# Gated networks of a two-block transformer: activation halves side by side in one 512-column product, summed on VectorE

## The reference

```
ff1, ff2:    (silu(h @ w_gate) * (h @ w_up)) @ w_down                      # 1024 -> 2816 -> 1024
glu1, glu2:  gu = u @ w_up                                                 # 1024 -> 2 x 3072
             gate = causal_dwconv(gu[..., :3072], conv_w) + conv_b         # 3 taps over the positions
             (silu(gate) * gu[..., 3072:]) @ w_down
```

## Time and profile before

| | us |
|---|---|
| median of 3 runs | 1452.08 |
| lowest, highest | 1450.59, 1460.54 |
| profiled execution | 1451.2 |
| its span | 1448.4 |
| TensorE busy in the span | 1343.1 |
| VectorE busy | 917.4 |
| ScalarE busy | 669.9 |

### The profile page before, as it was taken

The page is one execution under the profiler, slowest core; times in us unless marked ns, Lnnn a source line. Parts: engine busy times, 40 slices in busy tenths (PEclk is TensorE's granted clock), DMA queues, the critical chain, the costliest instruction groups (busy, mean ns, idle before and its releaser), DMA issues.

```text
span 1448.4 us, 24980 instructions
## 1 busy us (share of the span) xinstructions
PE 1343.1 (93%) x10130; PEld 1264.0 (87%) x10130; DVE 917.4 (63%) x1373; ACT 669.9 (46%) x983; POOL 110.8 (8%) x98
## 2 busy tenths in 40 slices
PE   5999979988799999779999999899998879899998
PEld 5999979987799999768899999799997769899997
DVE  5655556666555555666666666689895654666665
ACT  5443444555443434545445444467532333544443
POOL 1000010000100000340000000014001620000000
PEclk9999999999999999989999999999998989999999
DMA  6655543630255555330455455344340004355551
GB/s 258 220 186 176 196 161 120 233 117 1 102 175 177 195 179 184 125 128 4 143 198 180 174 180 197 117 146 155 138 145 31 30 30 175 137 183 176 195 195 71
DMA packets 30313, 214.85 MB, mean 148 GB/s; under 512 B 3488, under 2 KB 3616, under 8 KB 4768
## 3 DMA queue, kind: packets, MB, share of 16 engines
q1 hardware_dynamic: 29808, 212.23, 41.9%
q0 software_dynamic: 432, 1.57, 0.3%
HBM read 212.74 MB, written 1.05 MB: 148 GB/s over the span
## 4 chain that ended last, share of the span: by engine, by line
PE 80%; DVE 11%; ACT 3%; POOL 3%; issue 2%; DMA 1%; SPq 0%; DVEq 0%; POOLq 0%; ACTq 0%
PE bank L445 71%; DVE w_lo L1599 2%; PE bank L607 1%; POOL stat L1486 1%; PE bank L461 1%; PE bank L651 1%; ACT w_hi L1053 1%; POOL stat L1457 1%; PE bank L620 1%; DVE arena L1991 1%; ACT aT_hi L1071 1%; DVE par L1989 1%; DVE aT_lo L1620 1%; ACT arena L1241 1%; DMA pos_i<-positions 1%
## 5 line engine op out<-in xcount | busy, mean ns | idle before, releaser
L1599 DVE TENSOR_TENSOR w_lo<-raw,w_hi 128x2048 fp32r<-128x2048 f32 x199 | 458.2, 2303 | 229.5 <-ACT w_hi L1053 229.3
L445 PE MATMUL bank<-aT_hi,w_hi 128*128 128x256 f32 x1728 | 492.5, 285 | 4.5 <-DVE aT_lo L1620 3.9
L445 PE MATMUL bank<-aT_hi,w_lo 128*128 128x256 f32 x1728 | 490.3, 284 | 0.0
L445 PE MATMUL bank<-aT_lo,w_hi 128*128 128x256 f32 x1728 | 490.2, 284 | 0.0
L1053 ACT ACTIVATE w_hi<-raw 128x2048 fp32r<-128x2048 f32 x199 | 380.2, 1911 | 133.1 <-PE bank L445 131.2
L445 PEld LDWEIGHTS bank<-aT_hi,w_hi 128*128 128x128 f32 x1728 | 332.9, 193 | 8.0 <-issue 4.1
L445 PEld LDWEIGHTS bank<-aT_lo,w_hi 128*128 128x128 f32 x1728 | 333.0, 193 | 1.5
L445 PEld LDWEIGHTS bank<-aT_hi,w_lo 128*128 128x128 f32 x1728 | 332.8, 193 | 0.0
L445 PE MATMUL bank<-w_hi,aT_hi 128*128 128x256 f32 x592 | 172.2, 291 | 4.4 <-DVE aT_lo L1620 1.8
L445 PE MATMUL bank<-w_hi,hT_hi 128*128 128x512 f32 (+2 forms) x464 | 171.7, 370 | 1.9 <-DVE hT_lo L1714 1.9
L445 PE MATMUL bank<-w_hi,hT_lo 128*128 128x512 f32 (+2 forms) x464 | 171.4, 369 | 0.0
(11 more groups left out here) (309 smaller groups left out, 1331.1 us busy)
## 6 DMA issues: line engine op xcount, KB each, us to landing
raw<-weights SPq DMA_DIRECT2D x199, 1024.0 KB, 4.9
post_gain<-post_gains POOLq DMA_DIRECT2D x3, 512.0 KB, 4.2
residual<-x SPq DMA_DIRECT2D x2, 512.0 KB, 4.1
out<-residual SPq DMA_DIRECT2D x2, 512.0 KB, 2.6
par<-params SPq DMA_DIRECT2D x1, 837.0 KB, 7.5
con<-consts SPq DMA_DIRECT2D x1, 520.0 KB, 10.6
con<-consts SPq DMA_DIRECT2D x1, 64.0 KB, 6.2
pos_i<-positions SPq DMA_DIRECT2D x1, 1.0 KB, 7.3
```

The costliest lines, as they stand in the source:

```text
L445: last = nc.tensor.matmul(to, lhsT, rhs, start=start and n == 0, stop=stop and n == 2)
L1599: nc.vector.tensor_tensor(w_lo[:, i % 3, :], raw[:, i % 3, :], w_hi[:, i % 3, :].bitcast(f32), ALU.subtract).then_inc(w_lo_done, 1)
```

## The change

`aT_hi` and `aT_lo` become the two halves of one buffer. For each part and k, the rounded weight `w_hi` is multiplied by both at once, a moving operand of 2 x 256 columns, so that one half of a bank holds the sum over k of `w_hi` with `aT_hi` and the other that with `aT_lo`; then `w_lo` with `aT_hi` is added into the first half. A tile is now 16 products of 512 columns and 16 of 256. Gate and up have a bank each, `bank[4 + 2 * (f % 2) + part]`, so two tiles instead of four hold banks in turn. VectorE adds the two halves of each bank with a reduction over two elements, to `f_sum` (gate) and `f_up` in SBUF; ScalarE's and VectorE's later steps read these in place of the bank. ScalarE waits for the gate's sum (`gate_summed`) instead of the tile's products, and TensorE, before it writes a bank again, for the sum of the tile two before it. Down products, splits, the order of the items and everything outside the four networks stay.

```diff
--- before.py
+++ after.py
@@ -77,8 +77,8 @@
         w_lo = sb("w_lo", [128, 3, ITEM], f32r)
 
 
-        aT_hi = sb("aT_hi", [128, 8, SEQ], f32r)
-        aT_lo = sb("aT_lo", [128, 8, SEQ], f32r)
+        aT = sb("aT", [128, 2, 8, SEQ], f32r)
+        aT_hi, aT_lo = aT[:, 0], aT[:, 1]
 
         with nc.sbuf_tensor("z_silu", [128, 8, 512], f32) as z_silu:
             pass
@@ -142,6 +142,8 @@
         f_gate = room(2, SEQ)
         f_tanh = room(2, SEQ)
         f_hid = room(2, SEQ)
+        f_sum = room(2, SEQ)
+        f_up = room(2, SEQ)
 
         used[0] = 0
         proj = room(2, 2816)
@@ -252,6 +254,7 @@
 
         rows_ready, turned, turned_hi, turned_lo = sem("rows_ready"), sem("turned"), sem("turned_hi"), sem("turned_lo")
 
+        gate_summed, up_summed = sem("gate_summed"), sem("up_summed")
         gate_scaled, gate_conv, gate_tanh = sem("gate_scaled"), sem("gate_conv"), sem("gate_tanh")
         hid_ready, hid_hi, hid_lo = sem("hid_ready"), sem("hid_hi"), sem("hid_lo")
         y_done = sem("y_done")
@@ -487,17 +490,19 @@
                 def tile(f, i, q):
 
                     pe.wait_ge(w_lo_done, i + 1 + 6 * q)
-                    if f0 + f >= 4:
-                        pe.wait_ge(hid_ready, f0 + f - 3 + 4 * q)
-                    to = bank[4 + f % 4]
                     for part in range(2):
+                        to = bank[4 + 2 * (f % 2) + part]
+                        if f0 + f >= 2:
+                            pe.wait_ge(up_summed if part else gate_summed, f0 + f - 1 + 4 * q)
                         for k in range(8):
                             at = 1024 * part + 128 * k
                             if f == 0 and part == 0 and k % 2 == 0:
 
                                 pe.wait_ge(turned_lo, turn(name) + k // 2 + 1)
-                            last = exact(to[:, 256 * part:256 * part + 256], weights(i, at, at + 128), left(k),
-                                         k == 0, k == 7)
+                            hi, lo = weights(i, at, at + 128)
+                            nc.tensor.matmul(to[:, :].rearrange("p (a c) -> p a c", a=2), hi, aT[:, :, k, :],
+                                             start=k == 0, stop=False)
+                            last = nc.tensor.matmul(to[:, 0:256], lo, aT_hi[:, k, :], start=False, stop=k == 7)
                     last.then_inc(item_done, 1)
 
                 def down(m, i, q):
@@ -1102,9 +1107,8 @@
                 pre_norm(name)
 
                 def tile(f, i, q):
-                    gate = bank[4 + f % 4][:, 0:256]
-                    act.wait_ge(item_done, i + 1 + 6 * q)
-                    tanh_of = gate
+                    tanh_of = gate = f_sum[:, f % 2, :]
+                    act.wait_ge(gate_summed, f0 + f + 1 + 4 * q)
                     if conv:
                         tap = P("ffn_conv")[:, 72 * (name == "glu2"):72 * (name == "glu2") + 72]
                         bias = P("ffn_bias")[:, 24 * (name == "glu2"):24 * (name == "glu2") + 24]
@@ -1691,8 +1695,12 @@
                 tap = tap.rearrange("p (f t) -> p f t", t=3)
 
                 def tile(f, i, q):
-                    gate, up = bank[4 + f % 4][:, 0:256], bank[4 + f % 4][:, 256:512]
+                    gate, up = f_sum[:, f % 2, :], f_up[:, f % 2, :]
                     g = f_gate[:, f % 2, :]
+                    dve.wait_ge(item_done, i + 1 + 6 * q)
+                    for part, to, done in ((0, gate, gate_summed), (1, up, up_summed)):
+                        halves = bank[4 + 2 * (f % 2) + part][:, :].rearrange("p (a c) -> p c a", a=2)
+                        nc.vector.tensor_reduce(to, halves, AX.X, ALU.add).then_inc(done, 1)
                     if conv:
 
                         dve.wait_ge(gate_scaled, f0 - 44 + f + 1 + 4 * q)
```

## The result

The changed kernel takes 1472.29 us, the median of four runs (1471.05 to 1474.22), against 1453.03 for the kernel before beside it: the ratio is 1.0128, with a 95% interval of 1.0102 to 1.0155. It is slower by 1.3%. The forecast was 1466 with a range of 1450 to 1484, and gave slower by over 1% a chance of 0.46 and no change that a measurement tells 0.47; its own sum, 13.9 us, is just under 1%. The profiled execution took 1474.22 us, span 1472.3, which is 23.9 more than the span of the kernel before.

What follows compares the result with a forecast made beforehand. The prediction took TensorE as today's bound, with VectorE becoming the bound of glu1 and glu2. Terms +9.1 + 1.0 + 6.65 + 1.7 - 4.0 - 0.6 = +13.9 us on the 1452.1 median gave 1466, range 1450 to 1484.

Steps and rivals of the forecast that it cites:

- VectorE becomes the bound of the convolved networks: In glu1 and glu2, sums lengthen VectorE's tile from 5.95 to 7.64 us, its pair to 17.49, over TensorE's 16.58.
- TensorE's wait: In glu1 and glu2, TensorE waits for w_lo some 0.9 us a pair.
- Rival 1: Convolved networks: sums hidden, looped tile 7.0 us, TensorE stays the bound; -8 us in all, 1444; chance 0.08.
- rival 2: Convolved networks: sums dearer, 1.04 us each, pair 18.2 us; total 1488; chance 0.11.
- rival 4: Convolved networks: index work overlaps the first sum, no clock terms; tiles 7.4, pairs 17.0 us; total 1453; chance 0.15.
- the pitches of rows 2: TensorE's gate and up products: 227.5 and 120.0 ns by width, saving 12.5 ns per k, 0.20 us a tile.
- Rival 3: TensorE's alternating stream has no gain, plain networks save nothing: 1474 us, or 1472 by the skill's rule; chance 0.10.
- ff2: forecast -4.0: Network ff2: TensorE stays the bound, 22 tiles save 0.20 us each, -4.4; later last hT_lo costs +0.4.
- ff1: forecast -0.6: Network ff1: bank wait +1.1, clock +1.7, 19 tiles saving 3.8, end +0.4; together -0.6 us.
- The wait of tile 2 for its bank: In ff1, tile 2 waits for tile 0's gate sum, starting at 32.05: +1.1 us, plus +1.7 for the clock.
- glu1: forecast +10.1: Network glu1: VectorE's longer tiles delay the last down product by 9.1 us; slow-clock products there add +1.0.
- glu2: forecast +8.35: Network glu2: VectorE's longer tiles delay the last down product by 6.65 us; the clock after TensorE's idle adds +1.7.

Runs made afterwards that it cites:

- experiment 4: Changed kernel with its sums, banks and waits kept, but three products of 256 columns per k again instead of one of 512 and one of 256: 1479.57 us, ratio 1.0177.
- experiment 5: Changed kernel plus a third VectorE reduction of 512 constant values per tile, after hT_lo, with nothing waiting for it: 1498.75 us, ratio 1.0321.
- experiment 11: The change in the even tile of each pair only; the odd tile keeps three 256-column products and no sum: 1449.39 us, ratio 0.9987.
- experiment 9: Changed kernel with each weight transfer after the first three cut to its first 16 columns: 1470.87 us, one run.
- experiment 7: Changed kernel with the two halves of aT side by side for every k, so the 512-column operand is one piece: 1474.57 us, ratio 1.0135.
- experiment 12: Changed kernel with each bank's eight 512-column products first, then its eight of 256, so widths don't alternate: 1470.99 us, ratio 1.0126.
- experiment 1: The change in ff1 and ff2 only, glu1 and glu2 as in the kernel before: 1452.69 us, ratio 1.0002.
- experiment 3: Changed kernel's products and two banks without the VectorE sums, later steps reading each bank's first half: 1449.35 us, ratio 0.9978.
- experiment 6: Changed kernel with one hT_lo subtraction per convolved pair moved behind the next tile's sums, the other ahead of the down split: 1471.86 us, ratio 1.0115.
- experiment 2: The change in glu1 and glu2 only, ff1 and ff2 as in the kernel before: 1471.71 us, ratio 1.0131.
- experiment 10: The kernel before with each weight transfer after the first three cut to its first 16 columns: 1452.45 us, one run.
- second profile: The kernel before, unchanged, run once more to see the clock at the networks' starts: 1451.12 us.

## Why the prediction was right, and where it was off

**VectorE becomes the bound of the convolved networks: right, and shown.** Forecast: a tile of 7.64 and a pair of 17.49 us; measured 7.67 and 17.53. The price of a sum was taken from the score maximum, 690 ns, and is 684 ns (pitch 0.60 to 0.61 between queued ones). From the first sum to the convolution 1.69 us were added up and 1.71 measured (765.66 to 767.37), and for the rest of the tile 5.95 and 5.96: the terms are right one by one, not by errors that cancel. That the pace is VectorE's, experiment 4 (other products, same pair) and experiment 5 (a sum that nobody waits for, +1.22 a pair) show; that it becomes so only with the second tile's sums, experiment 11. TensorE's wait was put at 0.9 us a pair. By the pairs it is 0.74 (17.53 less 16.79), since the stream took 16.79 and not 16.58; the rows give 0.6 on the mean (11.6 / 19), since the record before a wait outlasts its pitch by 0.16. Rival 1 (sums hidden) and rival 2 (1.04 us a sum) are excluded by that one row, and rival 4 (light chain, pairs of 17.0) by the 17.53.

**The products: the term that was mis-sized.** The step "I take the pitches of rows 2, since both widths there run unbroken" gave 12.5 ns a k; alternating, the stream gave 6 to 7 in the pairs. Over the nine full-pitch pairs of ff2 that is 1.7 us in place of 3.6. Neither the transfers (experiment 9) nor the two-piece operand (experiment 7) hold it back; with the widths sorted it gives 11 (experiment 12). In the changed kernel I had seen 347 ns a k at the start of glu2, while no transfer ran, and took the transfers for the cause. Experiment 9 took that away, and so does the rest of that head: it stays at 347 ns with transfers at 117 GB/s. So the forecast pitch can be had by the alternating stream, and why the pairs run in the slower rhythm is open.

Rival 3 said that the stream has no gain at all and gave 1474 us, and the measured 1472.3 lies closest to it. Of its mechanism only half was there: the plain pairs did fall, by 0.19 us of the 0.40. The Trainium skill (TensorE: Matmul & The Clock Gate, section Back-to-back issue gap) gives N/2.4 + 2.5 ns as the gap of a single product in isolation, and about 131 ns a product for a stream of 512 columns; the prediction used the first for a stream. By it the saving is 2.5 ns a k. The runs show 6 alternating and 11 with the widths apart (360 to 349, experiment 12), and 227.5 ns a product in a stream of 512 columns, so neither figure fits these streams. The rival's total came close because of other terms, the heads and what lies between the networks; that is luck.

**ff2: forecast -4.0, measured 0.0.** The pairs gave 1.7 in place of 3.6. The end cost 0.6 (11.52 us from the last down but one to the end, 10.91 before) where 0.4 was forecast. And the head, which was to gain 0.8, lost 1.04 us (24.27 against 23.23), because the network began at the lower clock level: 0.50 in its first 4 us. I had no term for that. It isn't fixed to the change: with the same products in ff2, experiments 1, 3, 6 and 7 took 22.5 us there, 0.75 less than before, where the clock rose earlier, experiment 9 took 22.9 and experiment 5 24.3. With the old products and no sums it took 23.2 in all four traces (the kernel before twice, experiments 2 and 10).

**ff1: forecast -0.6, measured +0.2.** The wait of tile 2 for its bank (+1.1 and +1.7 for the clock) does not show in this profile, because TensorE began slowly: 19 products from 18.3 to 24.3 us, so that its second tile ended at 32.47, after the gate's sum (32.00). It shows in the profiles of experiments 1, 4, 5, 7, 9, 11 and 12, where tile 2 starts at 32.02 to 32.17 us after 0.7 to 2.0 us of idle; 32.05 was forecast. In experiment 4 (TensorE's timeline):

```profile
32.08 0.36 PE L503 MATMUL bank<-aT,w_hi 128*128 128x256 f32 x1 [1.96 <-DVE arena L1703]
```

With the products of the kernel before, and a start as fast as in its first profile (49 products from 18.3 to 24.3 us against 50), experiment 4 takes 25.42 us for the head against 24.14: the wait is worth +1.3 there. The clock's +1.7 is in none of the seven; the granted clock stays at 1.00 after the wait. The changed kernel's own head of 25.46 goes with its slow start: the kernel before took 25.82 in its second profile, with 28 products from 18.3 to 24.3. The pairs gave 1.7 of the expected 3.8 (19 x 0.20) and the end took 0.6.

**glu1: forecast +10.1, measured +12.3.** From the first sum on the forecast holds: the last down product starts 204.33 us behind it (717.08 to 921.41), where 203.74 was forecast. What was missed is the head. The first sum came 8.16 us after the first product in place of 5.95, as the first tile ran at the lower level (clock 0.50 in 706 to 713). Where the clock rose earlier, in experiments 2 and 7, glu1 takes 217.96 and 218.07 us against 207.72, +10.2 and +10.4, which is the forecast. For the last down item, of all slow products, I had taken +1.0 between 0 and 3.1; it is 7.51 in place of 7.17 us, +0.3, though TensorE had idled 6.4 us instead of 2. Nor does an idle of 2 us always cost the 1.7 us that the forecast read from the earlier trace rows: in experiment 3 TensorE idled 1.97 us there and the 24 products took 5.56. **glu2: forecast +8.35, measured +9.2**, and of that the clock term is +1.70 as forecast (7.16 us for the last 24 products, 5.46 before); the 0.9 above the forecast lies in tiles and pairs each some 0.05 us longer (7.20 for 7.15, 17.55 for 17.49).

**Between the networks**, 2.0 us more from ff2 to glu1, in code that both kernels share. The forecast had no term for it. The granted clock was lower there (PEclk third from the end, the kernel before and the changed one):

```profile
583.00:706.56 123.56, 99.47 (x706) 92.91 (x705) 76.24 (x162) 62.25 (x145) 29.00 (x18) 0.92 0.28 94
```

```profile
583.37:708.92 125.55, 101.35 (x702) 95.21 (x705) 76.10 (x162) 62.29 (x145) 29.00 (x18) 0.90 0.27 92
```

It doesn't look like chance: the four traces with the old products and no sums in ff2 took 123.5 to 123.6 us, and of the ten with either of them nine took 125.1 to 127.6 and one, experiment 5, 123.6. How the change in ff2 brings it on no run shows. The stretch from glu1 to glu2 took 324.2 us in both profiles and up to 10 more in others (experiments 3 and 6). So of the 10.0 us by which the profiles miss the sum (23.9 against 13.9), the pitch is 3.8 in the pairs of the two plain networks, and most of the rest is the clock level at the heads of networks and what lies between them. The medians are 19.3 us apart; the profiled execution of the changed kernel was 1.9 us above its own, that of the kernel before 1.8 below.

## What to carry to other kernels

Before you move work from the busiest engine to another, don't ask how busy that one is over the span, but how long its chain is for one turn of the loop in the stage that decides, with every handoff in it, and add the new work there. Here 63% busy hid a slack of under 2.5 us in 17: the first tile's sums were free, and the second's ran over it. A move like this need not be all or nothing: done for as many tiles as the slack holds, it costs nothing, and what it then gains should be weighed against the spread of the clock before more time goes into it.

## What was unexpected of the hardware

- Two widths of product in turn ran in one of two rhythms at full clock: 347 ns for 512 + 256 columns, in up to 56 k in a row at the head of a network, or a cycle of 350, 350 and 361 (353 on the mean) in the pairs; sorted by width they took 349 (230 + 119). Cutting the weight traffic from 187 to 1 GB/s changed the pairs of neither kernel.
- The same code took 324.0 to 334.4 us from glu1 to glu2 (nine of 14 traces 324.0 to 324.2), with a granted clock of 1.00 or 0.80 in one window of 50 us. Six runs of one kernel lay at 1462 and at 1472 with mean clocks of 0.968 and 0.960. That is more than the whole effect of the new products.
- A reduction of 512 values to 256 sums takes as long as one to 2 maxima (684 and 690 ns), from a bank or from SBUF (0.61 us to the next start). Outputs of 256 and of 2 values didn't differ.
